# Four one-hot places instead of two for two of three blocks, ScalarE's copies one group later, and one reload ten slots later

## The reference, cut to what matters

```python
def block(hb):                                   # hb: 128 tokens x 2048
    ...                                          # top-k by product keys: idx, gate (128 x 8 heads x 16)
    u = expert_u[idx]                            # one row of 2048 for each token and slot
    act = jax.nn.gelu(jnp.einsum('thkd,td->thk', u, hb).astype(jnp.float32), approximate=False)
    coef = (gate * act).astype(hb.dtype)
    return jnp.einsum('thk,thkd->td', coef, expert_v[idx])
```

## Time and profile before

| what | value |
| --- | --- |
| runs | 3747.65, 3736.11 and 3746.93 us, median 3746.93 |
| the profiled execution | 3736.59 us, its span 3734.9 us |
| mean granted TensorE clock | 0.905 of full speed |
| busy share of the span | PE 82%, DVE 63%, ACT 15%, POOL 27% |
| moved by DMA | 1351.61 MB, mean 362 GB/s |
| block 2's build, first one-hot to last store issued | 2411.75 to 2507.61 us |
| dense tiles | first 2061.19 us, last ends at 3564.71 us |

### The profile page before, as it was taken

How to read it: one execution, slowest core, us unless ns; L and a number is a source line. 1 busy time by engine, 2 the same in 40 slices (tenths; PEclk the granted TensorE clock), 3 DMA queues, 4 the chain that set the end, 5 groups by cost and what they waited for, 6 DMA issues and landing times.

```text
span 3734.9 us, 28635 instructions
## 1 busy us (share of the span) xinstructions
PE 3060.1 (82%) x9975; PEld 1838.6 (49%) x9975; DVE 2350.5 (63%) x3568; ACT 574.6 (15%) x1367; POOL 1019.7 (27%) x779
## 2 busy tenths in 40 slices
PE   4999998869996567797885898768999999999910
PEld 1333443733332434433664555556776667777710
DVE  3110114889995864557778767877756676665688
ACT  1000111121110444411244000150000000000001
POOL 3000001234333421124322322324332222222263
PEclk8999999989998778888886999989999999999965
DMA  9999655989999699989888999989999999999996
GB/s 312 394 362 369 246 191 182 350 314 402 408 340 376 234 381 409 399 326 363 322 311 318 413 416 417 415 269 416 417 402 420 420 420 419 420 419 417 417 416 233
DMA packets 314609, 1351.61 MB, mean 362 GB/s; under 512 B 26345, under 2 KB 75497, under 8 KB 194809
## 3 DMA queue, kind: packets, MB, share of 16 engines
q0 software_dynamic: 106912, 749.72, 50.1%
q1 hardware_dynamic: 155002, 559.79, 38.7%
q10 hardware_dynamic: 52552, 40.27, 3.4%
HBM read 1309.89 MB, written 38.96 MB: 361 GB/s over the span
## 4 chain that ended last, share of the span: by engine, by line
PE 39%; DMA 36%; DVE 14%; issue 7%; ACT 3%; POOL 1%; SPq 0%; DVEq 0%; ACTq 0%; POOLq 0%
DMA arena<-in_expert_v_dram,arena 18%; PE ps L1032 10%; PE ps L628 7%; DMA arena<-in_expert_v_dram 5%; DVE arena L2178 5%; PE ps L787 4%; PE ps L837 4%; DMA arena<-in_cache_k_dram 3%; PE ps L719 3%; DMA arena<-in_expert_u_dram,arena 3%; PE ps L586 2%; DVE arena L2098 2%; DMA arena<-in_w_ada_dram 2%; DMA arena<-in_w_in_dram 2%; PE ps L616 2%
## 5 line engine op out<-in xcount | busy, mean ns | idle before, releaser
L2178 DVE CUSTOM_DVE_ANT_0 arena<-arena 128x2048 f32<-128x2048 f32 x544 | 1242.1, 2290 | 333.9 <-DMA arena<-in_expert_u_dram,arena 328.7
L1032 PE MATMUL ps<-arena 128*128 128x512 f32 x3072 | 1360.5, 603 | 108.8 <-DMA arena<-in_expert_v_dram 53.6
L2450 POOL DMA_INDIRECT arena<-in_expert_u_dram,arena x544 | 762.6, 1402 | 1713.8 <-DVE arena L2178 1520.3
L1032 PEld LDWEIGHTS ps<-arena 128*128 128x128 f32 x3072 | 942.9, 309 | 520.9 <-issue 173.4
L2098 DVE SCALAR_TENSOR_TENSOR arena<-arena 128x2048 f32<-128x2048 f32 x158 | 371.6, 2352 | 210.5 <-issue 200.6
L837 PE MATMUL ps<-arena 128*128 128x512 f32 x896 | 409.2, 610 | 0.4 <-DVE arena L2029 0.2
L2450 POOL DMA_INDIRECT arena<-in_expert_v_dram,arena x160 | 214.4, 1340 | 431.1 <-DVE arena L2098 387.5
L586 PE MATMUL ps<-arena 128*128 128x128 f32 (+3 forms) x954 | 159.6, 321 | 173.6 <-DMA arena<-in_cache_k_dram 51.0
L628 PE MATMUL ps<-arena 128*128 128x512 f32 x640 | 291.2, 609 | 9.3 <-DMA arena<-in_w_in_dram 9.3
L837 PEld LDWEIGHTS ps<-arena 128*128 128x128 f32 x896 | 169.5, 194 | 245.1 <-issue 236.9
L586 PEld LDWEIGHTS ps<-arena 128*128 128x128 f32 (+3 forms) x954 | 129.3, 170 | 240.2 <-issue 81.9
(11 more groups left out here) (246 smaller groups left out, 1749.2 us busy)
## 6 DMA issues: line engine op xcount, KB each, us to landing
arena<-in_w_ada_dram SPq DMA_DIRECT2D x96, 1024.0 KB, 10.7
arena<-in_expert_v_dram SPq DMA_DIRECT2D x88, 1024.0 KB
arena<-in_expert_v_dram SPq DMA_DIRECT2D x168, 512.0 KB
arena<-in_w_in_dram SPq DMA_DIRECT2D x80, 1024.0 KB, 8.8
arena<-in_w_query_dram SPq DMA_DIRECT2D x36, 1024.0 KB
arena<-in_w_out_dram SPq DMA_DIRECT2D x32, 1024.0 KB, 5.0
arena<-dense_coefs SPq DMA_DIRECT2D x42, 768.0 KB
dense_coefs<-arena ACTq DMA_DIRECT2D x12, 2048.0 KB, 18.4
```

Source lines behind the costliest of these rows:

```text
L1032: ins = MM(ps[:, BANK[half, b] + c, :], weights, dense_v[m % V_DENSE][:, c * NC:(c + 1) * NC], start=(m == FIRST_TILE[half, b]), stop=(m = ...
L2178: V.tensor_tensor_reduce(out=u_slot[s % RING], in0=u_slot[s % RING], in1=h2[b], scale=1.0, scalar=0.0, op0=ALU.mult, op1=ALU.add, accum_ou ...
L2450: nc.gpsimd.indirect_dma_start(out=slot, out_offset=None, in_=table, in_offset=bass.IndirectOffsetOnAxis(ap=idx, axis=0),).then_inc(loaded ...
```

## The change

It has three parts.

1. Blocks 1 and 2 use four one-hot places. Two are the old ones; two more lie at `H20`, in the first 2048 words of what held block 0's tokens until slot 256. DVE waits for dot 256 before it writes there, and its one-hots of group n now wait for PE's group n-4. Block 0 keeps two places.
2. In all three blocks ACT's order becomes scale n, copy n-2, scale n+1, copy n-1: each copy moves behind the next group's scaling.
3. `T_LOW` goes from slot 430 to slot 440.

```diff
-T_LOW = 430
+T_LOW = 440
...
-        one_hot = [at(WS0 + 8 * P * i, 2, 4 * P) for i in range(2)]
+        one_hot = [at(off, 2, 4 * P) for off in (WS0, WS0 + 8 * P, H20, H20 + 8 * P)]
...
+        def hot_of(n):
+            return one_hot[n % (2 if n < QUADS else 4)]
...
-                    for q in range(QUADS + 1):
+                    for q in range(QUADS + 2):
                         if q < QUADS:
                             yield t_quad(b, q) + 0.2 * C_STEP[b]
                             n = QUADS * b + q
...
-                                hot = one_hot[n % 2][:, 0, i * P:(i + 1) * P]
+                                hot = hot_of(n)[:, 0, i * P:(i + 1) * P]
                                 A.activation(hot, hot, ACT.Copy, scale=slot_t[:, 0, 4 * q + i:4 * q + i + 1]).then_inc(hot_scaled, 1)
-                        if q == 0:
+                        if q < 2:
                             continue
                         yield t_quad(b, q) + 0.3 * C_STEP[b]
-                        n = QUADS * b + q - 1
+                        n = QUADS * b + q - 2
...
                     if b:
+                        dv.wait_ge(u_done, 2 * SLOTS)
                         dv.wait_ge(hot_used, QUADS * b)
                         dv.wait_ge(slots_turned, b)
...
-                        if n >= 2:
+                        if b == 0 and q >= 2:
                             dv.wait_ge(hot_used, n - 1)
+                        if b and q >= 4:
+                            dv.wait_ge(hot_used, n - 3)
```

More of the change, by code:

```diff
@@ L1023, in build_dense @@
                         for i in range(4):
-                            ins = MM(ps[:, n % 2, i * P:(i + 1) * P], one_hot[n % 2][:, 1, i * P:(i + 1) * P],
-                                     one_hot[n % 2][:, 0, i * P:(i + 1) * P], start=True, stop=True, skip_group_check=True)
+                            ins = MM(ps[:, n % 2, i * P:(i + 1) * P], hot_of(n)[:, 1, i * P:(i + 1) * P],
+                                     hot_of(n)[:, 0, i * P:(i + 1) * P], start=True, stop=True, skip_group_check=True)
                         ins.then_inc(hot_used, 1)
@@ L2065, in build_dense @@
                             dv.wait_ge(keys_split, b + 1)
-                        if n >= 2:
+                        if b == 0 and q >= 2:
                             dv.wait_ge(hot_used, n - 1)
+                        if b and q >= 4:
+                            dv.wait_ge(hot_used, n - 3)
                         wide = [P, 2, 4, P]
-                        V.tensor_tensor(one_hot[n % 2].rearrange("p i (t n) -> p i t n", n=P),
+                        V.tensor_tensor(hot_of(n).rearrange("p i (t n) -> p i t n", n=P),
                                         iota_key.unsqueeze(1).unsqueeze(1).broadcast_to(wide),
```

## The result

| | runs | median us | ratio to the runs of before on the same chip | 95% interval |
| --- | --- | --- | --- | --- |
| before | 12 | 3746.80 | | |
| the change | 12 | 3722.09 | 0.9941 | 0.9926 to 0.9956 |
| the change, second time | 12 | 3724.70 | 0.9953 | 0.9935 to 0.9972 |
| the change, third time | 7 | 3719.91 | 0.9948 | 0.9929 to 0.9966 |

The ratios are not the quotients of the medians, which for the first row of the change is 0.9934 (24.7 us); where ratio and medians differ, the ratio with its interval is what I go by. The change is faster by 0.5 to 0.6%, some 20 us. The forecast was 3725 us. The profiled execution took 3726.11 us with a span of 3724.1, only 10.8 under that of before, because the one of before had been a low one of its kernel (3736.59 against a median of 3746.8) and this one lies 4 us over its median.

What follows compares the result with a forecast made beforehand. After block 2's build, DMA bytes at 417 GB/s plus holes were taken to set the end. 18.0 + 1.5 - 5.0 + 2.0 = 16.5 us off 3736.59 gave 3720.1; half the gap to the median made 3725 us, range 3706 to 3743.

Steps and rivals of the forecast that it cites:

- What bounds the kernel: After block 2's build: the gather stream on a full DMA sets the end; PE's tiles have some 100 us to spare.
- Block 2's build: DVE's 19.4 us wait for PE goes, DVE becomes the bound, the longer end costs a little: 18.0 us gained.
- Block 1's build: Most of DVE's 24.9 us wait for PE is not to be had: 1.5 us gained.
- the pin: Block 1's build, 1996.78 us: a gelu in ACT's fixed order, behind ACT's copies of scores, holds DVE again.
- Block 0's build: Part 2 alone acts: PE's groups wait for copies now behind scalings, in and after the attention: 5.0 us lost.
- PE is on the path there: Block 0's attention: the head's transposes follow PE's group, so four groups waiting 0.57 us each for a copy cost 2.3 us.
- The lower sums: Slot 440: DVE's 24.05 us stall and the DMA hole after it go, PE waits about 20 us: 2.0 us gained.
- PE's 20 us reach the end: Rival: PE's new wait at the lower sums counts at the kernel's end; 3744 us, 3749 with half gap; chance 0.08.
- Another wait takes the place: Rival, block 2's build: DVE meets unlanded gathers or a busy staging place, half of 18 us stays; 3729 or 3734; chance 0.15.
- Block 1 gives all: Rival: all 24.9 us of DVE's wait in block 1's build go; 3702 us; chance 0.12.
- Slower: the copy behind the scaling: Rival: every group of blocks 0 and 1 pays 0.57 us, 36.5 us in all; 3753 us, 3758 with half gap; chance 0.05.
- The clock: After PE's new 20 us wait at the lower sums, a lower granted clock costs PE another 2.2 us, which falls into its reserve.

Runs made afterwards that it cites:

- e8: The change with T_LOW at 448 instead of 440, against the change: 3719.65 us, ratio to before 0.9947.
- e9: The change with block 2's one-hots written for one token of four only (result left incomplete): 3723.51 us, ratio to before 0.9955.
- e3: Part 1 alone against before: four places in blocks 1 and 2, copies in the old order, T_LOW 430: 3726.26 us, ratio 0.9962.
- e4: Part 2 alone against before: two places everywhere, copies two groups late, T_LOW 430: 3759.62 us, ratio 1.0057.
- e6: Parts 1 and 3 against before, that is the change with the old order of copies: 3719.58 us, ratio 0.9937.
- e7: The change with late copies in block 2 alone, blocks 0 and 1 in the old order: 3716.90 us, ratio to before 0.9946.
- e2: Parts 1 and 2 against before, that is the change with T_LOW back at 430: 3725.44 us, ratio 0.9961.
- e5: The change itself, unaltered, measured a second time against before: 3724.70 us, ratio 0.9953.
- e12: The change itself, unaltered, measured a third time against before: 3719.91 us, ratio 0.9948.
- e1: Part 3 alone against before: T_LOW 440, two places, copies in the old order: 3742.56 us, ratio 1.0002.
- e10: The change with three places instead of four in blocks 1 and 2 and late copies in block 2 alone: 3718.54 us, ratio to before 0.9938.
- e11: The change with late copies in block 2 alone, measured a second time: 3713.28 us, ratio to before 0.9925.

## Why the prediction was right, point by point

**What bounds the kernel.** That it is not PE is shown. From 424 to the end all fourteen traces take 1083 to 1089 us, whatever PE waits there (0 in before, 24.9 in the change, 69.4 in e8), while 256 to 424 goes from 771 to 816 with the builds, and the time with it. That the full DMA is the bound is read from its rate, 417 to 420 GB/s over nearly all of that stretch; no run moved fewer bytes.

**Block 2's build: 18.0 us.** The mechanism is right, the size too large. The build takes 80.9 us and not some 77, the store comes 12.8 us earlier; over the traces with four places and late copies the build is 78.5 to 81.0, against 95.9 and 99.8. The failed step is "I walked DVE's order through with no wait but that for group n-4": DVE's wait went as I said (2.1 us are left), but its order is not all that bounds. e9 shows that with less work on DVE the store's staging place comes next, and the end of the build takes 7.4 us from the last one-hots (2487.4) to the store, where I had counted 5.8. My walk also took PE's durations as given, and the rows of e3 and e4 show that they move with the granted clock. That part 2 is needed for it was my reading of the cycle, and it is wrong: e3 gets 11.4 of it with the old order.

**Block 1's build: 1.5 us.** 150.6 against 152.0, and 149 to 153 over the repeats: right in sum and wrong in its reason. I took the busy PE and the pin for the limit. e3, e6 and e7 show 145.5 to 146.1: part 1 alone gives 6 us here, and part 2 takes them away. The busy PE was no fixed limit: its 123.05 us become 116.17 in e3, at a granted clock of 0.86 and not 0.78, and 119.24 in the change at 0.83. I had put the clock's share at nothing. With early copies PE waits for scalings only (29.5 us in e3); with late ones it waits 26.6 us for copies and 5.2 for scalings. Its waits are together 2.3 us longer in the change than in e3 and its busy time is 3.1 us longer, which makes up the 5.2 us between the two builds.

**Block 0's build: 5.0 us lost.** Wrong, and the traces can settle it. Up to dot 248 the fourteen traces differ in one thing only, the order of ACT's copies in block 0: seven have it late (the change, e2, e4, e5, e8, e9, e12), seven as before (before, e1, e3, e6, e7, e10, e11). Means of the seven, in us between gelus:

| from the gelu of dots | late copies | as before | difference |
| --- | --- | --- | --- |
| 136 to 143 until 176 to 183 (attention) | 208.9 | 206.8 | 2.1 longer (0.4 to 3.8 by resampling) |
| 176 to 183 until 192 to 199 | 119.2 | 125.1 | 5.9 shorter (4.3 to 7.6) |
| 136 to 143 until 248 to 255 | 610.7 | 613.1 | 2.4 shorter (-0.3 to 4.5) |

There is a local loss in the attention, some 2 us and not 5, and more than that comes back right behind it: the second stretch is 117.5 to 120.9 us in every late trace and 123.2 to 128.8 in every other. It stands so in the traces of before and of the change:

```profile
1451.81:1577.66 125.85, 98.37 (x754) 53.13 (x754) 54.15 (x72) 60.47 (x148) 20.76 (x15) 0.88 1.00 403
1457.41:1575.84 118.43, 95.98 (x755) 50.95 (x754) 54.13 (x72) 60.02 (x148) 20.76 (x15) 0.93 1.02 414
```

The failed step is "PE is on the path there": the DMA share is 1.00 to 1.02 in this stretch, so what PE lost before it need not reach the end. Why late copies make the stretch shorter stays open; a higher granted clock (0.93 against 0.88) and rate (414 GB/s against 403) go with it.

**The lower sums: 2.0 us.** PE's new wait is 24.9 us where I had 20. The hole after 2740 did fill (420 GB/s), 3.5 us by my count. It is given back in the tail: from 3560 to the end of the span the DMA misses 164.1 - 175 x 282 / 417 = 45.8 us of full work, against 174.9 - 175 x 318 / 417 = 41.4 in before. The gathers run up to 42 us ahead and the last dots are only 12.5 us earlier, 11.4 of which come from the builds. By the traces part 3 is worth 0 to 1 us; the times put it at 3.5 us beside parts 1 and 2 (e2 against the change, interval by resampling 0.1 to 6.9), at 8.4 beside part 1 (e3 against e6, 1.6 to 15.0) and at 1.4 alone (-2.4 to 5.1). So it is a small gain beside four places by the times, which the traces hardly show, and alone its sign is not settled.

**The sum.** I had 18.0 + 1.5 - 5.0 + 2.0 = 16.5. The traces give about 14 us by dot 424 (777 on average with the change's builds, 792 with those of before) and 0 to 1 behind it; the times give 20, with 17 to 23 by resampling the 31 runs. That I came near rests in part on two errors that cancel, the build's 18 (3 too much) and block 0's loss of 5 (which did not come). The rest between traces and times, 5 to 6 us, is in part block 0's, 2 to 3 us by the table above; what is left is not explained, and two traces with the old builds are few.

There is luck in the 3725 too. I started from 3736.6 + 5.15 = 3741.7 us as the level of before. In the runs beside the first ones of the change that level was 3746.8, so my start was 5 us too low and my gain 8 too small against those medians (24.7), and the two left 3 us. Over all 74 runs of before on record the median is 3741.9, and there the start was right.

**The signs.** Several that I named were missed by little: DVE's wait is 2.1 us (under 2), the build 80.9 (under 80), its rate 333 GB/s (over 340), the span 3724.1 (near 3718). The last tile ends at 3582.2 and not near 3567, because PE waits longer and the build gave less. DVE's 24 us before the lower sums did go, and PE's wait came.

**The rivals.** "PE's 20 us reach the end" is shown wrong by e8. "Another wait takes the place" holds in part: 15 of 18 us came in the build's length, 12.8 at its last store. "Block 1 gives all" is wrong; 6 us are to be had there, with part 1 and early copies. "Slower: the copy behind the scaling" is the one whose mechanism I underrated: e4 measures it at 21 us with two places, in blocks 1 and 2 and not in block 0. It is harmless in block 2 only because of part 1.

**The clock.** After the wait of 24.9 us the granted clock is 0.71 in the next 9 us and 1.00 after, and after e8's 69.4 us it is 0.70 and 1.00. The rows of the change:

```profile
2755.33:2764.33 9.00, 9.00 (x15) 4.97 (x16) 8.93 (x16) 2.05 (x2) 5.75 (x4) 0.71 1.01 420
2764.00:2780.00 16.00, 16.00 (x39) 11.53 (x38) 14.90 (x28) 1.59 (x3) 9.00 (x6) 1.00 1.01 420
```

So PE works part of those 9 us at the 1.2 GHz level, and then at 2.4 GHz. That is 9 x 0.29 = 2.6 us, against the 2.2 of the prediction, and it fell into the reserve. The Trainium skill's rule that a gap costs TensorE more than its length ("TensorE: Matmul & The Clock Gate", section "HAM oscillation — how this bites in real kernels") agrees with these rows.

## What to carry to other kernels

When producer, scaler and consumer form a ring over a few places, add a place first and measure it alone: here the places alone gave as much as places and reordering together (0.9962 and 0.9961), and moving work behind other work on the scaler cost 21 us without them and with them some 5 us in block 1, where it wasn't needed. Cost such a reordering stage by stage: here it shortened block 2's build by 5 to 6 us and lengthened block 1's, and against no reordering at all (e6) even its best form shows no gain in the times. Don't take an engine's busy time as fixed when its waits change: PE's for the same 320 instructions was 64.3 to 80.5 us over these runs, with the granted clock at 0.93 to 0.78. In this kernel a wait on an engine with a reserve was free even at 69 us, and a stall that only shifted transfers in time was worth its hole in the DMA at most, and perhaps nothing once the tail had given it back.

## What was not expected of the hardware

In e9 the 2 MB store of a staging place that was issued at 2428.55 held its place until the copy at 2454.55, some 26 us, while the faster build fills the next place in 16 (2428.55 to 2444.53). With two staging places that is a next bound of the build. From dot 424 on the length of the kernel stayed within 6 us over all traces, while the stages before dot 256 varied by 18 us (the gelu of dots 248 to 255 at 1848.7 to 1867.0) between kernels that are the same there or nearly: much of the spread of the profiled executions arises before the first dense tile. And PE's clock is part of a ring's price: in block 1's build the same 560 instructions took PE 122.3 to 123.1 us in the three traces with two places (granted clock 0.78 to 0.80) and 116.2 to 118.2 in the five with more places and early copies there (0.84 to 0.86).
